# Last expert step: VectorE adds the even value rows, TensorE the odd ones, and its rows go through seven slots

## What is computed

```python
def block(ub):                                   # ub: 128 tokens x 2048
    q = (ub @ w_q).reshape(128, 8, 2, 128)       # 8 heads
    s = einsum('thpk,hpnk->thpn', q, sub_keys)
    ...                                          # per head: the 16 best of 128*128 experts: eid; g = softmax
    act = gelu(einsum('td,tkd->tk', ub, peer_u[eid]))
    return einsum('tk,tkd->td', g * act, peer_v[eid])
x = LN2(ALPHA * x + (1 + gate2(c)) * PEER(u2))
```

## Time and profile before

| what | us |
|---|---|
| median of 3 runs (2929.33 to 2932.17) | 2930.45 |
| the profiled execution | 2932.28 |
| its span, first to last instruction | 2930.5 |
| PE busy | 2456.9 (84%) |
| DVE busy | 1717.8 (59%) |
| ACT busy | 649.2 (22%) |
| POOL busy | 700.1 (24%) |

### The profile page before, as it was taken

How to read it: one execution, slowest core, us unless ns; L and a number is a source line. 1 busy time by engine, 2 the same in 40 slices (tenths; PEclk the granted TensorE clock), 3 DMA queues, 4 the chain that set the end, 5 groups by cost and what they waited for, 6 DMA issues and landing times.

```text
span 2930.5 us, 37003 instructions
## 1 busy us (share of the span) xinstructions
PE 2456.9 (84%) x13796; PEld 1710.6 (58%) x13796; DVE 1717.8 (59%) x3151; ACT 649.2 (22%) x908; POOL 700.1 (24%) x798
## 2 busy tenths in 40 slices
PE   5799999999999999998967777777777877777777
PEld 2489999999998999997832222222333322222223
DVE  1147767868778654545565555555575655555541
ACT  0132333323332453336320111110011101111100
POOL 2301110010010000000133333333343433333331
PEclk8679999999999999998989999999999999999999
DMA  8857776675785545553699999999999999999995
GB/s 285 293 181 272 239 269 202 227 271 193 236 275 186 173 149 165 165 153 108 236 376 422 421 422 422 422 422 422 421 422 422 393 421 422 422 421 422 422 421 208
DMA packets 209534, 910.31 MB, mean 311 GB/s; under 512 B 18629, under 2 KB 18629, under 8 KB 134149
## 3 DMA queue, kind: packets, MB, share of 16 engines
q0 software_dynamic: 111776, 713.34, 60.5%
q1 hardware_dynamic: 97611, 194.98, 20.7%
HBM read 902.09 MB, written 7.86 MB: 311 GB/s over the span
## 4 chain that ended last, share of the span: by engine, by line
PE 54%; DMA 37%; DVE 5%; issue 3%; POOL 1%; ACT 0%; POOLq 0%; SPq 0%; DVEq 0%; ACTq 0%
DMA vRing<-in_peer_v,idxV 33%; PE ps L555 13%; PE ps L559 12%; PE ps L557 12%; PE ps L795 10%; PE ps L579 2%; DMA modRing<-in_w_mod 2%; DMA uRow<-in_peer_u,idxU 1%; DVE uRow L1654 1%; PE ps L499 1%; PE ps L530 1%; DVE acc L1316 1%; DMA raw<-in_w_in 1%; PE ps L542 0%; PE ps L591 0%
## 5 line engine op out<-in xcount | busy, mean ns | idle before, releaser
L795 PE MATMUL ps<-vRing,diag 128*128 128x512 f32 x2304 | 1062.7, 606 | 353.3 <-DMA vRing<-in_peer_v,idxV 340.6
L795 PEld LDWEIGHTS ps<-vRing,diag 128*128 128x128 f32 x2304 | 419.4, 191 | 995.0 <-issue 888.9
L1654 DVE SCALAR_TENSOR_TENSOR uRow<-uRow,ps 128x2048 f32<-128x2048 f32 x288 | 655.5, 2287 | 513.5 <-DMA uRow<-in_peer_u,idxU 487.3
L555 PE MATMUL ps<-actH,wH 128*128 128x288 f32 x2816 | 851.6, 302 | 27.9 <-DVE actL L1214 13.7
L557 PE MATMUL ps<-actL,wH 128*128 128x288 f32 x2816 | 838.1, 298 | 0.0
L559 PE MATMUL ps<-actH,wL 128*128 128x288 f32 x2816 | 835.2, 297 | 0.0
L1242 DVE TENSOR_TENSOR wL<-raw,wH 128x1024 fp32r<-128x1024 f32 x352 | 429.2, 1223 | 388.2 <-ACT wH L839 386.5
L555 PEld LDWEIGHTS ps<-actH,wH 128*128 128x128 f32 x2816 | 535.3, 190 | 44.6 <-issue 31.8
L559 PEld LDWEIGHTS ps<-actH,wL 128*128 128x128 f32 x2816 | 537.3, 191 | 0.0
L839 ACT ACTIVATE wH<-raw 128x1024 fp32r<-128x1024 f32 x352 | 372.6, 1060 | 741.0 <-PE ps L559 703.8
L557 PEld LDWEIGHTS ps<-actL,wH 128*128 128x128 f32 x2816 | 536.3, 190 | 0.1
(11 more groups left out here) (206 smaller groups left out, 965.7 us busy)
## 6 DMA issues: line engine op xcount, KB each, us to landing
raw<-in_w_in SPq DMA_DIRECT2D x224, 512.0 KB, 4.3
restRing<-in_w_mod POOLq DMA_DIRECT2D x128, 512.0 KB, 5.5
modRing<-in_w_mod POOLq DMA_DIRECT2D x64, 512.0 KB, 5.9
raw<-in_w_b_out SPq DMA_DIRECT2D x32, 512.0 KB, 3.6
raw<-in_w_a_out SPq DMA_DIRECT2D x32, 512.0 KB, 3.6
raw<-in_w_o SPq DMA_DIRECT2D x32, 512.0 KB, 3.6
raw<-in_w_q SPq DMA_DIRECT2D x32, 512.0 KB, 3.7
uRow<-in_peer_u,idxU POOLq DMA_INDIRECT x288, 16.5
```

What stands on the lines that cost most here:

```text
L555: nc.tensor.matmul(out, wh, actH[:, kc, :], start=(kc == 0), stop=False, skip_group_check=True)
L795: mm = nc.tensor.matmul(ps[:, 4 + n, :], diag[:, k, :], vRing[:, k % 4, n * 512:(n + 1) * 512], start=(first and k == 0), stop=True, skip_ ...
L1654: V.scalar_tensor_tensor(out=row, in0=row, scalar=1.0, in1=ps[:, 0:4, :].rearrange("p b n -> p (b n)"), op0=ALU.mult, op1=ALU.mult, accum_ ...
```

## The change

Only the last step (step 17, of tile t = 2) is changed.

- Value rows with even k are added by VectorE into an SBUF accumulator `mixed` (= `uRing[0]`): row 0 by a multiply with its weight, rows 2, 4, ... 14 by a fused multiply-add. A new semaphore `v_mixed` counts them. Then VectorE multiplies `mixed` with the gate `g2P` and adds `x1Tok[2]`. These instructions stand ahead of `take_sum(2)`.
- Value rows with odd k are added by TensorE as before, in a loop of their own; `take_sum(2)` waits for 8 fewer rows on `v_done`, and `residual2` adds `mixed` in place of `x1Tok[2]`.
- The 16 gathers go through seven slots in turn (`last_row(k)`, k % 7): four of `vRing`, then `uRing[1]` to `uRing[3]`. Gathers 0 to 3 wait as before. Gathers 4 to 6 wait for the dot product that last used the buffer. Gather k from 7 on waits until row k - 7 has been added, on `v_mixed` or `v_done` by who adds it. Their order in POOL's queue is by k.
- ScalarE still writes all 16 diagonals.

```diff
--- before.py
+++ after.py
@@ -290,6 +290,7 @@
         wts_ready = sem("wts_ready")
         diag_ready = sem("diag_ready")
         v_done = sem("v_done")
+        v_mixed = sem("v_mixed")
         f_free = sem("f_free")
         fs_ready = sem("fs_ready")
         folded = sem("folded")
@@ -312,6 +313,15 @@
 
         def group(c, lo=0, hi=N):
             return ps[:, bass.ds(bank_set(c), 4), lo:hi]
+
+        LAST_RING = 7
+
+        def last_row(k):
+
+            n = k % LAST_RING
+            if n < 4:
+                return vRing[:, n, :], v_in[n], 16 * (4 * (STEPS - 1) + k // LAST_RING + 1)
+            return uRing[n - 3][:, :], u_in[n - 3], 16 * (4 * STEPS + k // LAST_RING + 1)
 
         def raw_count(c, u):
 
@@ -479,7 +489,18 @@
                 step(2 * i + 1, 1)
             pool.wait_ge(idxv_ready, STEPS)
             for k in range(TOPK):
-                gather_v(STEPS - 1, 1, k)
+                slot, landed, n = last_row(k)
+                if k < 4:
+                    pool.wait_ge(v_done, TOPK * (STEPS - 1) + k - 3)
+                elif k < LAST_RING:
+                    pool.wait_ge(dot_done, TOPK * (STEPS - 1) + 10 + k)
+                elif (k - LAST_RING) % 2 == 1:
+                    pool.wait_ge(v_done, TOPK * (STEPS - 1) + (k - LAST_RING) // 2 + 1)
+                else:
+                    pool.wait_ge(v_mixed, (k - LAST_RING) // 2 + 1)
+                pool.indirect_dma_start(slot, None, peer_v,
+                                        bass.IndirectOffsetOnAxis(ap=idxV[:, 1, k:k + 1], axis=0))\
+                    .then_inc(landed, 16)
             pool.wait_ge(state_out, 16)
 
         @block.tensor
@@ -816,7 +837,16 @@
                     if t + 1 == SAMPLES:
                         pe.wait_ge(rep_ready, 3)
                     turn_u2(t + 1)
-                add_experts(b, False)
+                if t < 2:
+                    add_experts(b, False)
+            for k in range(1, TOPK, 2):
+                slot, landed, count = last_row(k)
+                pe.wait_ge(diag_ready, TOPK * (STEPS - 1) + k + 1)
+                pe.wait_ge(landed, count)
+                for n in range(4):
+                    mm = nc.tensor.matmul(ps[:, 4 + n, :], diag[:, k, :], slot[:, n * 512:(n + 1) * 512],
+                                          start=False, stop=True, skip_group_check=True)
+                mm.then_inc(v_done, 1)
 
         @block.scalar
         def _(act):
@@ -1676,7 +1706,7 @@
             def take_sum(t):
 
                 m = ROWS[t]
-                dve.wait_ge(v_done, TOPK * (TILES[t][1] + 1))
+                dve.wait_ge(v_done, TOPK * (TILES[t][1] + 1) - (TOPK // 2 if t == 2 else 0))
                 at_least(dve, y_out, 16 * t)
                 if t == SAMPLES:
                     V.tensor_copy(fin[:, :], ps[:, 4:8, :].rearrange("p b n -> p (b n)")).then_inc(fs_ready, 1)
@@ -1691,7 +1721,7 @@
                 f = fin[0:m, :]
 
                 def residual2():
-                    chain.link(V.tensor_tensor(f, f, x1Tok[t][0:m, :], ALU.add))
+                    chain.link(V.tensor_tensor(f, f, (x1Tok[t] if t < 2 else uRing[0])[0:m, :], ALU.add))
                     chain.all()
 
                 def statistics():
@@ -1740,6 +1770,20 @@
                     step(b - 1, 0)
                     step(b, 1, more=False)
             chain.restart()
+            mixed = uRing[0]
+            for k in range(0, TOPK, 2):
+                slot, landed, count = last_row(k)
+                dve.wait_ge(landed, count)
+                if k == 0:
+                    V.tensor_scalar(mixed[:, :], slot, wts[:, 1, 0:1], None, ALU.mult).then_inc(v_mixed, 1)
+                else:
+                    dve.wait_ge(v_mixed, k // 2)
+                    V.scalar_tensor_tensor(out=mixed[:, :], in0=slot, scalar=wts[:, 1, k:k + 1],
+                                           in1=mixed[:, :], op0=ALU.mult, op1=ALU.add).then_inc(v_mixed, 1)
+            dve.wait_ge(v_mixed, TOPK // 2)
+            chain.link(V.tensor_tensor(mixed[:, :], mixed[:, :], g2P[:, :], ALU.mult))
+            chain.all()
+            chain.link(V.tensor_tensor(mixed[:, :], mixed[:, :], x1Tok[2][:, :], ALU.add))
             take_sum(2)
             for piece in finish(2):
                 piece()
```

## The result

| | median us | runs | ratio to before, 95% interval |
|---|---|---|---|
| before | 2930.45 | 5 (2929.33 to 2933.24) | |
| changed | 2916.49 | 5 (2914.67 to 2918.18) | 0.995 (0.994 to 0.9961) |

The account below looks back on a forecast made before the run. The prediction took TensorE to bound the last step's value rows. Row 3 landing at 2864.92, twelve rows at 2.485 us and VectorE's tail put the final sum at 2899.4, 14.4 us earlier: median 2916.0 us, range 2912.5 to 2922.

Parts of the forecast that it names:

- The bound: Last step's value rows: TensorE-bound at 3.45 us per row against 2.485 for fetching one.
- Row 0's multiply: VectorE's first row in the last step, a multiply by a column: 1.25 us, at most 2.35.
- The fused rows: VectorE's seven rows with an accumulator in the last step: 2.35 us each.
- Gather 3 held: POOL's gather 3, held by VectorE's row 0 until 2860.16 instead of 2859.28, makes later rows 0.88 us late.
- Row 3's landing: Last step's row 3 lands at 2864.92: gather start 2858.34 + 5.7 + 0.88 us.
- the stream between row 3 and row 15: Last step's gathers: twelve more rows at 2.485 us after row 3, row 15 landing at 2894.74.
- the 0.9 us that TensorE was to be ahead: Before the final sum: TensorE done 0.9 us before VectorE, which releases the sum at 2899.4.
- Gathers held later cost nothing: POOL's gathers from 4 on are issued 6.8 us or more before due; gather 5, held, ends 5.0 us before.
- The slots: Last step's gather buffers: a cycle needs 10.7 us; four slots give 9.9, seven 17.4.
- rival E: TensorE's clock at 0.50 in the whole last stage: rows of 6.9 us, 2931.6 us, no gain; chance 0.03.
- B: Last step's stream does better: gather 3 not held, gap ahead of it partly closed; 2913.5 us, chance 0.06.
- D: Last step's stream stays at 3.43 us per row for a reason other than TensorE: 2927.4 us, chance 0.04.

Follow-up runs that it names:

- the doubled operations: The changed kernel with a second fused operation of the same form on VectorE behind rows 2 to 12: interval 48.11 us, median 2915.98 us.
- the third profile: The changed kernel run a third time with nothing altered: interval 49.52 us from last dot product to final sum, median 2916.48 us.
- the two kernels by turns: The changed kernel with gathers alternating v and u slots, 2914.14 us; then also gate and residual applied behind row 10, 2914.1 us.
- the first profile: The changed kernel as first measured: interval 48.73 us from last dot product to final sum, median 2916.49 us.
- first kernel by turns: The changed kernel with its seven slots, gathers taking a v and a u slot alternately: interval 46.72 us, median 2914.14 us.

## Why the prediction was right

**The bound** was TensorE, as said; the kernel with slots alone has the same 62.05 us as before.

**The terms.** Row 0's multiply: 1.25 us estimated from the slope of two short forms, 1.29 measured. The fused rows: 2.35, measured 2.35. Gather 3 held: 1.82 forecast, 1.83 measured. Row 3's landing: 6.58 us after its gather began, measured 6.5 (2860.68 - 0.13 - 2854.03). The hold by a multiply by a column had no row before; the changed kernel has it (gather 3), and the kernel with row 0 on ScalarE shows it gone. The rule from the Trainium skill, "SBUF — State Buffer", section "Who interferes with whom", that I leaned on there is borne out, for this form too. The bound of about 358 GB/s for transfers from HBM, from the Trainium skill's "DMA: Bandwidth & Descriptors", section "Where 436 GB/s comes from", isn't: 421 GB/s in the last step.

**What was mis-sized** is the stream between row 3 and row 15: 12 x 2.485 = 29.8 us forecast, 31.8 measured (2892.51 - 2860.68). Rows 5 to 14 keep the pace of 2.485; the rest is row 4 (0.8 late behind the restart) and row 15 (1.1 to 1.2 late). Because row 15's delay is more than the 0.9 us that TensorE was to be ahead, TensorE and not VectorE released the final sum. The interval should have been 2899.4 - 2851.8 = 47.6 and was 48.7; the gain 14.4, measured 13.3 in the interval and 14.0 in the medians. That the median came within 0.5 us of the forecast is therefore partly luck: the interval was 1.1 to 1.9 us longer than summed in all three profiles, and the medians' chance differences took up the rest.

**Gathers held later cost nothing**, as followed through; the doubled operations show that there was more room than I had thought. I named gather 5 as the one that meets row 2. It began 0.03 us after that operation's start and went through in 0.94 us; gather 6 was held in its place.

**The slots.** That they would be needed was said, with 10.7 us for a cycle against 9.9. Measured it is 12.1, with two rows at the lower clock among them, and what I left out is the row that is issued beside each gather. The conclusion stood because seven slots have room for either.

**The clock** (rival E) did fall, which I had given 0.03 and only for the whole stage: TensorE's row 3 took 5.37 us with the clock at 0.50 from 2861 to 2864, ahead of it two idle times of 1.27 and 1.98 us. It cost nothing there: row 5's data landed at 2866.4, 0.4 us after row 3 was done. I had counted a clock under 1 among the signs of being wrong; in the third profile it fell in row 15 and did cost 1.7 us. In the two kernels by turns, with 1.3 us of idle time before every row, it didn't fall.

**The other rivals**: B (2913.5) is near what the kernels by turns (2914.1) reach, by its two mechanisms: gather 3 isn't held there and the gap ahead of it is closed. D is out by the 421 GB/s.

**Open**: why row 15 is late in the changed kernel (three profiles of three) and in none of the kernels with five slots, doubled work, row 0 on ScalarE or slots by turns. In the first profile its data are moved except for a small rest at about 2890, and it lands at 2892.4:

```profile
2890.00:2891.00 1.00, 0.11 (x1) 0.00 (x0) 1.00 (x1) 0.00 (x0) 0.00 (x0) 1.00 0.19 66
2891.00:2892.00 1.00, 0.00 (x0) 0.00 (x0) 0.97 (x2) 0.00 (x0) 0.00 (x0) 1.00 0.05 8
```

A DMA share of 0.05 is about one engine of sixteen. Such a tail doesn't make a row late by itself: in the first kernel by turns the share is 0.39, 0.14 and 0.04 from 2888 to 2891, and its row 15 lands at the pace, at 2891.2. The trace doesn't name the engine, and none of these kernels separates the causes. Open too is why the restart behind the held gather was slow in two profiles of the changed kernel and not in the third.

## What to carry to other kernels

Where an engine has no idle time in a stage and the next bound is near, moving a part of its work is enough: four of sixteen rows brought 11.1 us and eight 13.0. Count a slot's cycle with the transfers that are queued ahead of its own, not with the unqueued latency; buffers added beyond that count bring nothing unless the order of issue lets them be filled earlier, which brought another 1.5 to 2.3 us here (46.72 against 48.25 and 49.01). And ask of a held gather what is on order behind it: the one that met an empty queue cost 0.4 to 1.4 us for a hold of 0.9, those with rows on order nothing.

## What the runs showed of the hardware

- A multiply by a column, from SBUF to SBUF at 0.63 ns per element (1.29 us for 2048), holds a GpSimd-issued gather that begins beside it until 0.80 us after its end, just as a fused operation with two SBUF inputs does. Dot products with one input in PSUM don't: the gather at 2844.09 in the changed kernel, beside the one from 2842.53 to 2844.82, took 0.94 us.
- A gather that begins 0.03 to 0.04 us behind a VectorE operation's start wasn't held: gather 5 of the changed kernel (2857.41, row 2 at 2857.38) took 0.94 us, and so did that of its two other profiles and of the kernels with five slots and doubled work. One that began 0.15 us behind such a start was held (3.01 us, in the kernel with row 0 on ScalarE).
- At full rate, a row of 1 MB landed every 2.485 us whether five or seven slots fed the stream; with four it was 329 GB/s from 2870 to 2890 and 3.02 us.
- A clock fall early in a row makes it 5.35 to 5.37 us instead of 3.67. It came eight times in six profiles (two each with four slots and in the third profile of the changed kernel), each time behind an idle time of TensorE of 1.92 to 2.44 us. Other rows behind idle times of as much and more (2.40, 2.77 and 3.11 us) kept their 3.67.
